# Scan angles, sines and preparations of a two-layer hybrid decoder moved to other slots, with the state one token further and the mix without scaling of p2

## What is computed

```
ar, ai = exp(lr*dt) * cos(li*dt), exp(lr*dt) * sin(li*dt)        # S5: one complex factor a per state
h[t] = a * h[t-1] + B u[t];   y[t] = Re(C h[t]) + d * u[t]       # B, C complex, 16 channels per group
...
p = softmax(s);  p = p[:, :, 0] - lam * p[:, :, 1]               # differential attention, two maps per head
o = rms(p @ v, out_gain) * (1 - lambda_init)                     # then gated with silu(z)
```

## Time and profile before

| | |
|---|---|
| median of 3 runs | 952.34 us (951.09 to 952.35) |
| the profiled execution's own time | 952.75 us, span of its instructions 951.0 us |
| TensorE busy | 936.0 us, 98% of the span |
| VectorE, ScalarE, GpSimd busy | 610.0 (64%), 575.4 (60%), 111.3 us (12%) |
| granted TensorE clock | full speed in all 40 slices |
| transfers | 165.83 MB, 174 GB/s on the mean |

### The profile page before, as it was taken

One profiled execution on the slowest core, in us unless ns is written; L12 is line 12 of the kernel. 1 busy time (PEld: TensorE's weight loads), 2 busy tenths in 40 slices (PEclk: granted clock), 3 DMA queues, 4 the chain that ended last, 5 costly groups with the idle time before them and its releaser, 6 DMA issues.

```text
span 951.0 us, 15769 instructions
## 1 busy us (share of the span) xinstructions
PE 936.0 (98%) x5939; PEld 796.3 (84%) x5939; DVE 610.0 (64%) x971; ACT 575.4 (60%) x928; POOL 111.3 (12%) x126
## 2 busy tenths in 40 slices
PE   7999999999999999999999999999999999999998
PEld 7998888778878999888888788888888888888886
DVE  4688889799797954855644555555555555555553
ACT  4689886876967746544545573555456545554332
POOL 3101002011020000000002540220021002200000
PEclk9999999999999999999999999999999999999999
DMA  8776544445343467555999986668999866654662
GB/s 285 185 190 196 156 133 134 136 135 175 112 140 127 137 198 266 179 192 190 175 166 180 195 239 169 182 174 160 171 160 172 197 175 178 176 175 156 212 213 85
DMA packets 116007, 165.83 MB, mean 174 GB/s; under 512 B 19301, under 2 KB 56298, under 8 KB 115690
## 3 DMA queue, kind: packets, MB, share of 16 engines
q1 hardware_dynamic: 99504, 159.67, 64.0%
q10 hardware_dynamic: 16442, 5.33, 2.3%
HBM read 162.86 MB, written 2.11 MB: 173 GB/s over the span
## 4 chain that ended last, share of the span: by engine, by line
PE 82%; ACT 7%; DVE 6%; issue 3%; DMA 1%; POOL 1%; ACTq 0%; SPq 0%; DVEq 0%
PE bank L456 21%; PE bank L458 21%; PE bank L457 21%; PE bank L483 3%; PE bank L484 3%; PE bank L485 3%; ACT wh L969 2%; ACT res L1078 2%; PE bank L600 1%; ACT res L1090 1%; DVE wl L977 1%; ACT scr L1230 1%; DVE scr L1747 1%; PE bank L592 1%; DMA res<-in_x 1%
## 5 line engine op out<-in xcount | busy, mean ns | idle before, releaser
L977 DVE TENSOR_TENSOR wl<-raw,wh 128x1024 fp32r<-128x1024 f32 x295 | 362.0, 1231 | 252.7 <-ACT wh L969 251.5
L969 ACT ACTIVATE wh<-raw 128x1024 fp32r<-128x1024 f32 x295 | 310.5, 1058 | 190.2 <-PE bank L458 119.5
L456 PE MATMUL bank<-wh,xh 128*128 128x512 f32 x768 | 307.1, 400 | 0.3 <-DVE wl L977 0.3
L458 PE MATMUL bank<-wh,xl 128*128 128x512 f32 x768 | 300.0, 391 | 0.0
L457 PE MATMUL bank<-wl,xh 128*128 128x512 f32 x768 | 299.2, 390 | 0.0
L458 PEld LDWEIGHTS bank<-wh,xl 128*128 128x128 f32 x768 | 144.1, 188 | 31.1
L456 PEld LDWEIGHTS bank<-wh,xh 128*128 128x128 f32 x768 | 144.3, 188 | 29.0 <-DVE wl L977 0.7
L457 PEld LDWEIGHTS bank<-wl,xh 128*128 128x128 f32 x768 | 144.5, 188 | 27.7
L456 PE MATMUL bank<-wh,yh 128*128 128x512 f32 x256 | 100.5, 393 | 0.0
L458 PE MATMUL bank<-wh,yl 128*128 128x512 f32 x256 | 99.7, 390 | 0.0
L457 PE MATMUL bank<-wl,yh 128*128 128x512 f32 x256 | 99.6, 389 | 0.0
(11 more groups left out here) (317 smaller groups left out, 1022.4 us busy)
## 6 DMA issues: line engine op xcount, KB each, us to landing
raw<-in_o_w_in SPq DMA_DIRECT2D x128, 512.0 KB
raw<-in_e_w_in SPq DMA_DIRECT2D x130, 256.0 KB, 3.3
raw<-in_e_w_out SPq DMA_DIRECT2D x32, 512.0 KB
raw<-in_o_w_out SPq DMA_DIRECT2D x32, 512.0 KB
raw<-in_e_w_in SPq DMA_DIRECT2D x31, 512.0 KB
raw<-in_s_w_glu SPq DMA_DIRECT2D x8, 512.0 KB
res<-in_x SPq DMA_DIRECT2D x8, 256.0 KB, 6.8
res<-in_x SPq DMA_DIRECT2D x1, 2048.0 KB, 9.6
```

Source lines behind the costliest of these rows:

```text
L456: nc.tensor.matmul(o, l_hi, w_hi, start=first, stop=False)
L458: mm = nc.tensor.matmul(o, l_lo, w_hi, start=False, stop=last)
L969: nc.scalar.activation(wh[:, j % RING, :], raw[:, j % RING, :], ACT.Copy).then_inc(hi_done, 1)
L977: nc.vector.tensor_tensor(wl[:, j % RING, :], raw[:, j % RING, :], wh[:, j % RING, :].bitcast(F32), ALU.subtract).then_inc(lo_done, 1)
```

## The change

- Angles go from slot 0 to slots 7 and 8 of the step before (one part each), the sines from slot 1 to slot 11.
- The other preparations on VectorE go behind the split of their slot (`s5_ahead`): powers in slots 9 and 12, `far` in 11 and 13, `skip` in 10.
- The state is taken one token further: B is multiplied by powers 1 to 4 of a instead of 0 to 3, and C by 0 to 3 instead of 0 to 4. Power 0 needs no product, so `s5_far` computes three powers instead of five, and ScalarE copies C and B themselves (`s5_own`, four copies, slot 10).
- `s5_hold` goes to ScalarE: eight copies of 64 columns instead of one VectorE product of 512 (slot 10).
- `s5_low` of all four pairs goes to slots 10, 11, 13 and 15 of the last stretch.
- The mix leaves the maps unscaled: p1 + p2 * (-lam * l1 / l2) with the sums l1, l2. The following norm divides l1 out again, for which GpSimd multiplies its epsilon by l1 squared (two more operations per head).

```diff
-TAB_SLOT, FAR_SLOT, BA_SLOT = [0, 0], [-7, -4], [-10, -4]
+TAB_SLOT, FAR_SLOT, BA_SLOT = [-9, -8], [-5, -3], [-7, -4]
-NEAR_SLOT, HOLD_SLOT, SKIP_SLOT = [-1, 2], -3, -8
+NEAR_SLOT, HOLD_SLOT, SKIP_SLOT, OWN_SLOT = [-1, 2], -3, -6, -6
+TABLE_SLOT = -5
+LOW_SLOT = {10: 0, 11: 1, 13: 2, 15: 3}
...
                     pe.wait_ge(cc_done, 2 * i + 2)
+                    pe.wait_ge(b0_done, i + 1)
-                        nc.tensor.matmul(o[0:32, at:at + 64], ba[:, r, t, 0:32],
-                                         cc[r][:, t, 0:HOP, :].rearrange("p k h -> p (k h)"), start=r == 0, stop=False)
+                        nc.tensor.matmul(o[0:32, at:at + 64], b0[:, r, t, :],
+                                         cc[r][:, t, :, :].rearrange("p k h -> p (k h)"), start=r == 0, stop=False)
...
-                            mm = nc.tensor.matmul(tokens_at(h, k, e, 1), ca[:, r, TH * h + e, 32 * (k + 1):32 * (k + 2)],
+                            mm = nc.tensor.matmul(tokens_at(h, k, e, 1), ca[:, r, TH * h + e, 32 * k:32 * k + 32],
...
+            def s5_own(i):
+                if i:
+                    act.wait_ge(y_ps, i)
+                    act.wait_ge(near_ps, 2 * i)
+                else:
+                    act.wait_ge(zeros, 2)
+                    act.wait_ge(bc_b, 1)
+                    act.wait_ge(bc_c, 4)
+                for r in range(2):
+                    nc.scalar.activation(cc[r][:, :, 0, :], bc_all[:, i, 2 + r, :].rearrange("p (i h) -> p i h", h=16), ACT.Copy)
+                for g in range(2):
+                    at = slice(64 * g, 64 * g + 64)
+                    ins = nc.scalar.activation(b0[at, :, :, 16 * g:16 * g + 16],
+                                               bc_all[at, i, 0:2, :].rearrange("p r (i h) -> p r i h", h=16), ACT.Copy)
+                ins.then_inc(b0_done, 1)
+            def s5_hold(i):
+                act.wait_ge(h_done, 2 * i) if i else act.wait_ge(prm_exp, 3)
+                for t in range(TB):
+                    ins = nc.scalar.activation(mg[:, t, :], later, ACT.Copy, scale=mag_all[:, TB * i + t:TB * i + t + 1])
+                ins.then_inc(hold_done, 1)
             def s5_pad(i, r):
+                act.wait_ge(b0_done, i + 1)
-                    dst = ca[at, r, :, :].rearrange("p i (k h) -> p (i k) h", k=5)[:, :, 16 * g:16 * g + 16]
+                    dst = ca[at, r, :, :].rearrange("p i (k h) -> p (i k) h", k=HOP)[:, :, 16 * g:16 * g + 16]
...
-                    if TAB_SLOT[1] + 1 == at:
+                    if TABLE_SLOT == at:
                         table(i)
+                    if OWN_SLOT == at:
+                        s5_own(i)
+                    if HOLD_SLOT == at:
+                        s5_hold(i)
...
             def powers():
-                v.memset(pr[:, 0, :], 1.0)
-                v.memset(pi[:, 0, :], 0.0)
...
-                link(v.tensor_scalar(nlam, nlam, LAMBDA_INIT, None, ALU.add))
+                link(v.tensor_scalar(nlam, nlam, LAMBDA_INIT, -1.0, ALU.add, ALU.mult))
...
-                    x = bc_all[:, i, 2 + f, :].rearrange("p (i k h) -> p i k h", k=1, h=16).to_broadcast([P, TB, 5, 16])
-                    y = pw[:, k, :, a_].rearrange("p k (i h) -> p i k h", h=1).to_broadcast([P, TB, 5, 16])
+                    x = bc_all[:, i, 2 + f, :].rearrange("p (i k h) -> p i k h", k=1, h=16).to_broadcast([P, TB, HOP - 1, 16])
+                    y = pw[:, k, 1:HOP, a_].rearrange("p k (i h) -> p i k h", h=1).to_broadcast([P, TB, HOP - 1, 16])
-                times(cc[r], r, 0)
+                o = cc[r][:, :, 1:HOP, :]
+                times(o, r, 0)
-                flat_of = "p i k h -> p (i k h)"
-                v.tensor_tensor(cc[r].rearrange(flat_of), cc[r].rearrange(flat_of), ca_t.rearrange(flat_of),
+                v.tensor_tensor(*(x.rearrange("p i k h -> p i (k h)") for x in (o, o, ca_t)),
-            def s5_hold(i):
-                x = mag_all[:, TB * i:TB * i + TB].rearrange("p (i c) -> p i c", c=1).to_broadcast([P, TB, NCH])
-                y = later.rearrange("p (i c) -> p i c", i=1).to_broadcast([P, TB, NCH])
-                link(v.tensor_tensor(mg[:, :, :], x, y, ALU.mult))
             def s5_powers(i, r):
-                    y = pw[:, k, 0:HOP, a_].rearrange("p s (i h) -> p i s h", h=1).to_broadcast([P, TB, HOP, 16])
+                    y = pw[:, k, 1:HOP + 1, a_].rearrange("p s (i h) -> p i s h", h=1).to_broadcast([P, TB, HOP, 16])
...
             def rotate_out(i, h):
+                    dve.wait_ge(hold_done, i + 1)
...
+                    for h in range(2):
+                        if IN_SLOT[h] == at:
+                            rotate_in(i, h)
+                        if OUT_SLOT[h] == at:
+                            rotate_out(i, h)
+            def s5_ahead(n, s):
+                for i in range(DA_PAIRS):
+                    at = s5_at(n, s, i)
...
-                    if at == HOLD_SLOT:
-                        s5_hold(i)
-                    for h in range(2):
-                        if IN_SLOT[h] == at:
-                            rotate_in(i, h)
-                        if OUT_SLOT[h] == at:
-                            rotate_out(i, h)
-                    if HIGH_SLOT + 1 == at:
-                        s5_low(i)
+                if n == DA_PAIRS and s in LOW_SLOT:
+                    s5_low(LOW_SLOT[s])
...
-                link(v.reciprocal(rec[:, k:k + 4], lsum[:, k:k + 4]))
-                link(v.tensor_scalar(rec[:, k + 2:k + 4], rec[:, k + 2:k + 4], nlam, None, ALU.mult))
+                link(v.reciprocal(rec[:, k + 2:k + 4], lsum[:, k + 2:k + 4]))
+                link(v.scalar_tensor_tensor(out=rec[:, k:k + 2], in0=lsum[:, k:k + 2], scalar=nlam, in1=rec[:, k + 2:k + 4],
+                                            op0=ALU.mult, op1=ALU.mult))
-                    ins = v.tensor_scalar(p2, p2, rec[:, k + 2 + t:k + 3 + t], None, ALU.mult)
-                link(ins)
-                for t, o, w in ((0, T, P), (1, 0, T)):
-                    p1, p2 = s_sb[:, 2 * h, o:o + w], s_sb[:, 2 * h + 1, o:o + w]
-                    ins = v.scalar_tensor_tensor(out=p1, in0=p1, scalar=rec[:, k + t:k + t + 1], in1=p2,
-                                                 op0=ALU.mult, op1=ALU.subtract)
+                    ins = v.scalar_tensor_tensor(out=p1, in0=p2, scalar=rec[:, k + t:k + t + 1], in1=p1,
+                                                 op0=ALU.mult, op1=ALU.add)
...
                         split_lo(dve, 2 * i + (CH_DA + c), j + LEAD)
+                        s5_ahead(i, s)
...
                 split_lo(dve, CH_Z + s // UNITS, s % UNITS + LEAD)
+                s5_ahead(DA_PAIRS, s)
...
             def out_norm(a, h):
+                pool.wait_ge(p_exp, score_no(a, 2 * h) + 1)
+                l, x = lsum[:, 4 * h:4 * h + 2], rno[:, 2 * h:2 * h + 2]
+                if a:
+                    pool.wait_ge(y_ready, head_no(a - 1, h) + 2)
+                link(g.tensor_tensor(x, l, eps, ALU.mult))
+                link(g.tensor_tensor(x, x, l, ALU.mult))
                 pool.wait_ge(pv_ssq, head_no(a, h) + 1)
-                link(g.tensor_tensor(sso[:, 2 * h:2 * h + 2], sso[:, 2 * h:2 * h + 2], eps, ALU.add))
+                link(g.tensor_tensor(sso[:, 2 * h:2 * h + 2], sso[:, 2 * h:2 * h + 2], x, ALU.add))
```

More of the change, by code:

```diff
@@ L262, in build @@
         bt = [flat[:, 4096 + 512 * k:4608 + 512 * k].rearrange("p (a h) -> p a h", a=GP) for k in range(2)]
-        ca_t, *cc = [flat[:, at:at + 640].rearrange("p (i k h) -> p i k h", i=TB, k=5) for at in (3072, 3840, 4480)]
+        ca_t = flat[:, 3072:3456].rearrange("p (i k h) -> p i k h", i=TB, k=HOP - 1)
+        cc = [flat[:, at:at + 512].rearrange("p (i k h) -> p i k h", i=TB, k=HOP) for at in (3840, 4480)]
         ba_t = [x.rearrange("p r n -> p (r n)").rearrange("p (i s h) -> p i s h", i=TB, s=HOP) for x in prod]
@@ L276, in build @@
         keep = res.rearrange("p t n -> p (t n)")
-        ca = keep[:, 0:2560].rearrange("p (r i k h) -> p r i (k h)", r=2, i=TB, k=5)
-        near = keep[:, 2560:3584].rearrange("p (i n) -> p i n", i=TB)
+        ca = keep[:, 0:2048].rearrange("p (r i k h) -> p r i (k h)", r=2, i=TB, k=HOP)
+        near = keep[:, 2048:3072].rearrange("p (i n) -> p i n", i=TB)
+        b0 = keep[:, 3072:3584].rearrange("p (r i h) -> p r i h", r=2, i=TB)
         pw = keep[:, 3584:3904].rearrange("p (r k i) -> p r k i", r=2, k=5)
@@ L315, in build @@
             ("t_ps", "xin_sb", "near_ps", "near_sb", "x_ps", "x_read", "h_done", "y_ps"))
+        b0_done, hold_done = sem("b0_done"), sem("hold_done")
         gelu_done, s5_hi, s5_lo, v_out = sem("gelu_done"), sem("s5_hi"), sem("s5_lo"), sem("v_out")
```

## The result

| | before | after |
|---|---|---|
| median of 20 runs each | 951.86 us | 954.16 us (ratio 1.0023, 95% interval 1.0016 to 1.003) |
| profiled execution, span | 951.0 us | 953.5 us |
| first product of unit 3, still in the set-up | 69.86 | 71.09 |
| first product of the gate, after the scan | 353.02 | 355.53 |
| the stretch between these two | 283.16 | 284.44 |

A forecast was written before the change was run, and what follows sets the result against it. TensorE, busy 98% of the span, bounds the kernel; at most 3.7 us of waits can be won. Step 0 +2.5, step 1 +0.7, steps 2 and 3 -0.25 each, last pair -0.15, memsets -0.1: +2.4, median 954.7, range 951.0 to 957.6.

The forecast's parts named there:

- The parts that help: TensorE's waits at the first head's `y_turn` (1.23, 1.23, 0.3) go; shorter pads win 0.22 a pair, 0.15 in the last.
- The mix: VectorE's mix, slots 4 and 7: 0.58 us shorter per head, not on TensorE's path there.
- The first step: Pair 0, nothing to win: normalised rows 1.15 us late at slot 12, TensorE 2.5 late in all by slot 14.
- ScalarE's block in slots 10 and 11: ScalarE's work from `gelu` to the split of slot 11, `hold` and `s5_own` included: 12.3 us, `wh` ready at 219.95.
- the wait of 0.6 ahead of the split of slot 11: VectorE waits 0.6 us for ScalarE's `wh` in slot 11, in all four steps.
- Slots 12 and 14 as the only places to look: Asked only whether preparations are done at slots 12 and 14; steps 1 to 3 come 1.2 us late at slot 14.
- the whole list from slot 4: VectorE's work from the split of slot 4 to the second powers, steps 1 to 3: 34.2 us, before 32.7.
- Costed at nothing: GpSimd's two operations per head, moved low parts, waits for `b0`, `hold`, `dd`: 0; uncovered 0.5 a head and 2 us.
- B: Rival, no change: `wh` is punctual in slot 11, only VectorE's list late (1.9 step 0, 0.6 others); 952.4, chance 0.24.
- C: Rival, faster: second powers done before TensorE reaches slot 14 in every step; 948.7, chance 0.14.
- D: Rival: ScalarE's block is longer than its rows, 1 us more in each of four steps; 958 to 959, chance 0.08.
- E: Rival: the second head's GpSimd operations hold VectorE up, 0.4 in each of three steps; 955.9, chance 0.04.

The follow-up runs named there:

- a_hold10: The changed kernel with `hold` on ScalarE in slot 10 instead of slot 13; median 954.61 us, ratio 1.0036 to the kernel before.
- a_angles0b: The changed kernel with the angles back in slot 0, ahead of the split, and the table in slot 1; 950.72 us, ratio 0.9984 to the kernel before.
- a_far13: The changed kernel with both `far` parts in slot 13, first powers in slot 10 (pair 0: slot 6); 948.38 us, ratio 0.9967 to the kernel before.
- a_back: The changed kernel with `hold` back on VectorE (slot 13, one product) and the low parts on their old place; 952.89 us, ratio 1.001.
- a_oldmix: The changed kernel with the old mix and GpSimd's norm without its two new operations; 955.36 us, ratio 1.0037 to the kernel before.
- a_angles0: The changed kernel with the angles back in slot 0, behind the split, and the table in slot 1; 980.03 us, ratio 1.0292 to the kernel before.

## Why the prediction came out as it did

The side was right, and so was the half of the mechanism that is VectorE's own list; the half that is ScalarE's block was not, and that the time came so near, 954.7 against 954.16, is luck. The sum had +2.4, the change itself costs 1.3, and about 1 us of the measured 2.3 is a difference that two sets of runs of the same code show too.

- *The parts that help*: right in size. First head's `y_turn` -3.0 (forecast -2.76), the input product behind the shorter pads -0.84 (-0.8). The mix, counted inside VectorE's list, is worth 1.6 to 1.8 by itself; the rest of the change therefore costs 2.9 to 3.1. No run undoes the state's one token with its copies (`s5_own`) alone; what that part is worth by itself stays open.
- *The first step*: `qk_turn` 1.14 late, forecast 1.15 (its own subtraction, 100.15 less 99.07, gives 1.08). `s5_turn` then 0.75 more, forecast 1.35, the difference being the wait below.
- *ScalarE's block in slots 10 and 11*: this step failed. It counted `hold`, which stands in slot 13, so `wh` was there in time and the wait of 0.6 ahead of the split of slot 11 came in none of the four steps. The price of `hold` was right: 2.02 us against 1.9. By the Trainium skill (ScalarE: Activation LUTs, What ACT_TABLE_LOAD costs) the estimate for it had been 1.9 to 2.0; the trace agrees. The rest of the block was right, too: from `gelu` (211.17) to the end of ScalarE's split of slot 11 (221.44) 10.3 us, against 12.3 less 1.9. Where `hold` does stand in slot 10 (a_hold10), the wait is 0.59 in the first step but only 0.17 in the third; the losses of a step come out at the forecast all the same, because VectorE's own part is larger there (next point).
- *Slots 12 and 14 as the only places to look*: incomplete. The same lateness meets TensorE first at the second head's `y_turn` in slot 11, 0.47 in each of three steps. There the prediction asked when the norm was there, not when TensorE wanted the head. Together slots 11 and 14 lost 0.87 a step, forecast 1.2, of which 0.6 were VectorE's own. Where the other 0.27 comes from is shown in part: against TensorE's own starts VectorE's split of slot 4 came 1.2 us earlier than before the change, not 1.4, and each stall costs TensorE some 0.15 more than its bracket.
- *What made `s5_turn` late*: the prediction added up the whole list from slot 4, 34.2 us, and the sum held to 0.1. But a_angles0b shows that this list is no single path: without the angles it idles in slot 9 and ends no earlier against TensorE. What counts at slot 14 is what stands behind the squares of slot 9, 14.9 us instead of 11.55: the first powers, moved there from slot 6, and `far`'s first part. Moving those, with pair 0's, removes the waits of L516, L569 and L671 (a_far13); how much of it is `far` and how much the powers was not separated.
- *Costed at nothing*: right for `hold` and the low parts on VectorE (a_back); the last low part cost 0.36 at the gate: it stands in slot 15 as before, but behind the split now (354.79, the split at 353.64). The prediction's cover names only the three low parts that move to other slots.
- *Rivals*: the condition of B is what happened, `wh` in time, and its 1.9 in the first step was exact; 0.87 instead of its 0.6 in the three later steps and the 0.36 at the gate make +1.2 out of its +0.05, and +1.28 was measured. C came true only with other slots (a_far13). D falls because the block took what its rows had said, E with a_oldmix.

## What to carry to other kernels

Find all instructions of the engine that sets the time (TensorE here) that wait for another engine's list, in the order in which it reaches them; the lateness is paid at the first one, and what is left at the next. Before adding up a list, look for the places where it starts anew behind another engine: work removed ahead of such a place becomes idle time, work moved behind it is paid in full. And compare a stretch between two instructions of the trace, when the ends of the program scatter by as much as the change is worth.

## What the runs showed of the hardware

In a_angles0 TensorE stood still for 5.5 us ahead of 200.25 (third step), and behind it the granted clock was 0.50 (1.2 GHz). The columns of these windows are the stretch, its length, the busy time and count of the engines, then clock and transfers:

```profile
180.00:193.00 13.00, 12.96 (x106) 10.38 (x106) 5.62 (x9) 7.41 (x15) 0.00 (x0) 1.00 0.23 72
193.00:200.00 7.00, 1.74 (x8) 1.11 (x6) 4.84 (x10) 6.95 (x19) 0.39 (x2) 0.93 0.12 32
200.00:204.00 4.00, 3.75 (x36) 3.29 (x37) 3.93 (x13) 3.94 (x11) 0.00 (x0) 0.50 0.71 224
```

Products of 512 columns followed each other every 0.43 us until 205.7, and every 0.23 from 206.0 on:

```profile
203.18 0.63 PE L463 MATMUL bank<-wh,xl 128*128 128x512 f32 x1
203.61 0.63 PE L461 MATMUL bank<-wh,xh 128*128 128x512 f32 x1
...
206.02 0.40 PE L461 MATMUL bank<-wh,xh 128*128 128x512 f32 x1
206.25 0.39 PE L462 MATMUL bank<-wl,xh 128*128 128x512 f32 x1
```

Subtracted start by start from the changed kernel, this stall cost 2.5 us beyond its own length, and one of 4.1 us in the first scan 2.8. The waits of up to 0.99 us in the changed kernel's scan left the clock at 1.00.

In the set-up GpSimd copies 512 columns twice (1.18 us from 59.08), and two of VectorE's operations on 32 columns beside it took 0.61 and 0.51 instead of 0.19:

```profile
59.14 0.61 DVE L1597 SCALAR_TENSOR_TENSOR scr<-scr 128x32 f32<-128x32 f32 x1
59.79 0.51 DVE L1598 TENSOR_SCALAR scr<-scr 128x32 f32<-128x32 f32 x1
60.33 0.19 DVE L1599 TENSOR_TENSOR scr<-scr 128x32 f32<-128x32 f32 x1
```

The copies make the difference and not the kind of the operations, as a_hold10 shows: there the copies start at 60.00, L1598 takes 0.18, and the operations at 60.09 and 60.73 take 0.61 and 0.53. The Trainium skill (SBUF — State Buffer, Who interferes with whom) says of a VectorE operation with two inputs in SBUF that it contends with a GpSimd operation that reads SBUF. The trace agrees for the first of the two rows; the second has one tensor as input, which this sentence does not cover. In the scan, where GpSimd's operations have two columns, no such thing is seen in VectorE's list.
